# One tile of the normed rows kept in PSUM for the first mixer stage of a two-layer trunk

## The chip, the cores and the metric

The kernel runs on one core of a Trainium2 chip. The metric is the device time of one execution in microseconds (us); the median of three runs is compared. Engines are named as in the profile: PE is the matmul engine, PEld its weight load, DVE the vector engine, ACT the scalar engine, POOL GpSimd, SP the engine that only issues DMAs. A queue is written as SPq or POOLq.

## The reference, cut to what matters

The trunk has two layers over 512 positions of width 1024. Each layer sums three token mixers (A: banded attention with a learned position bias, B: a recurrent block, C: differential attention), merges them by gates, norms the result, and then runs PEER, which looks up 128 experts for each position (8 heads of 16):

```python
def peer_ffn(h, w_q, sub_keys, u, v):
    ...
    hid = jax.nn.gelu(jnp.einsum('td,thkd->thk', xb, u[experts]))
    return jnp.einsum('thk,thkd->td', g * hid, v[experts])
```

So each expert of each position costs a dot of the position's normed row `xb` with a gathered row `u` of 1024 floats, and then a weighted addition of a gathered row `v`. The scores of mixer A are

```python
    s = jnp.where(valid[None, :, None, None, :], s + bias[None, None], NEG_INF)
    p = jax.nn.softmax(s, axis=-1).astype(v.dtype)
```

## The kernel before

The sequence is cut into two halves of 256 positions, and each half runs through both layers: four phases, s = 0 to 3 (phases 0 and 1 are the halves in layer one, 2 and 3 in layer two). A half is two tiles of 128 positions, t = 0 and 1. All data are 32-bit floats.

In each phase PE, ACT and DVE go through the stages A, B, C, G (merge gates), O (output projection) and T (choice of experts). The experts' work of a phase does not end in it: part of it, gathering included, is strewn over the mixer stages of the next phase. The list `ITEMS` gives the order of all gathered rows: "P" is a pair of u and v rows, "U" and "V" single ones. `row_plan` says how many of them stand at each place of the stages. POOL runs ahead through the list and gathers each row (128 positions, 4 KB each, 512 KB in all) by an indirect DMA into a slot of a ring. In stage A the ring has 16 to 20 slots of one row. POOL waits until the slot's old row has been used.

DVE takes the rows in the same order. A "U" row is one dot, L1196, in which both inputs lie in SBUF: the gathered row and `hp[:, t, :]`, the normed rows of tile t. Stage A of phases 1 to 3 holds 76 rows: 16 ahead of its first maximum, then three behind each of the four maxima of a unit, and three behind the unit's diagonals.

Stage A has four units u of two heads. A unit has four score maps i = 2m + t (head m of the pair, tile t). PE writes a map (L629 bias, L632 scores, L635 mask), DVE takes its maximum (L1443), ACT its exponential (L953). When all four are done DVE makes the reciprocals of the sums (L1451) and four diagonal matrices (L1458), with which PE transposes and normalises the maps (L656, "weighing"); then come the outputs (L674, L676) and the q and k projection of unit u + 2 (L581 in `project_qk`). The four maps lie in four PSUM banks, 2 to 5. The V projection (L611 in `project_v`) follows the scores of unit 0. In phases 1 and 3 a map has 384 or 512 keys, in phases 0 and 2 it has 128 or 256.

The engines run their programs strictly in order:

```python
            def maxima(kind, s, u):
                ...
                for i in range(4):
                    dve.wait_ge(s_done[kind], n * 4 + i + 1)
                    v.tensor_reduce(nmax[:, u % 2, i:i + 1], sc[i][:, 0:nk(s, i % 2)], X, ALU.max, negate=True
                                    ).then_inc(smax[kind], 1)
                    rows((s, kind, u, i))
```

SP loads the weights as 512 KB panels into seven slots. Ahead of the q and k panels of unit 2 (and of unit 3) it loads a bias strip, for which it waits until all scores of unit 0 (of unit 1) are done (L498). At the end of a phase the sums of the experts' v rows lie in banks 4 to 7; DVE adds them up (L1217), and only then does PE turn the next half's rows (L593).

Of the kernel before, what the change touches and what calls it, by code (L numbers as in the profile page):

```python
# [216 lines left out]
for _n in PE_SUMS:  # L217
    GROUP_ROWS.setdefault((sum_group(_n), ITEMS[_n][4]), []).append(_n)

# [31 lines left out]
def trunk(nc, t_in, out):  # L251
    with ExitStack() as ctx:
# [113 lines left out]
        bank = [ctx.enter_context(nc.psum_tensor(f"bank{i}", [P, 512], F32)) for i in range(8)]  # L366
        sc = bank[2:6]
        tp = bank[6:8]
        pa = bank[4:8]
# [50 lines left out]
        tables = sem("tables")  # L420

# [29 lines left out]
        def nk(s, t):  # L451
            return (2 * (s % 2) + t + 1) * P
# [118 lines left out]
        def _(pe):  # L571
# [43 lines left out]
            def scores(kind, s, u):  # L615
# [7 lines left out]
                for i in range(4):  # L623
                    m, t = divmod(i, 2)
                    if u:
                        pe.wait_ge(e_done[kind], (n - 1) * 4 + i + 1)
                    k = nk(s, t)
                    if kind == "A":
                        mm(sc[i][:, 0:k], ident, strip[:, u % 2, m, STRIP - k:STRIP], start=True, stop=False)  # L629
                    rows = slice(m * HEAD_DIM, (m + 1) * HEAD_DIM)  # L630
                    for lo, hi in pairs_of(s, t):
                        mm(sc[i][:, lo:hi], qt[rows, u % 2, t * P:(t + 1) * P],  # L632
                           kt(lo // HALF, kind, u)[rows, 0:hi - lo], start=(kind == "C"),
                           stop=(kind == "C" and hi < k))
                    mm(sc[i][:, k - P:k], ident, maskblk, start=False, stop=True).then_inc(s_done[kind], 1)  # L635
# [71 lines left out]

# [174 lines left out]
        def _(act):  # L882
            fn = nc.scalar.activation
            copy = nc.scalar.copy

            def gelus(key):

                for n in rows_of(key):
                    p, kind, head, k, t = ITEMS[n]
                    c = head * TOP + k  # L890
                    if kind == "V" and n in PE_PLACE:
# [56 lines left out]
            def exps(kind, s, u, maps=range(4)):  # L948
                n = s * UNITS + u
                for i in maps:  # L950
                    k = nk(s, i % 2)
                    act.wait_ge(smax[kind], n * 4 + i + 1)
                    fn(ex[:, i * SEQ:i * SEQ + k], sc[i][:, 0:k], ACT.Exp, bias=nmax[:, u % 2, i:i + 1],  # L953
# [170 lines left out]
            for s in range(PHASES):  # L1124
                take_turned(xt, bank[0:2], x_turned, x_taken, s * 4)
# [43 lines left out]
        def _(dve):  # L1169
# [10 lines left out]
            def rows(key):  # L1180

                for n in rows_of(key):
# [12 lines left out]
                    if kind != "V":  # L1195
                        v.tensor_tensor_reduce(row, row, hp[:, t, :], 1.0, 0.0, ALU.mult, ALU.add, hid[:, t, c:c + 1]  # L1196
# [242 lines left out]
            def maxima(kind, s, u):  # L1439
                n = s * UNITS + u  # L1440
                for i in range(4):
                    dve.wait_ge(s_done[kind], n * 4 + i + 1)
                    v.tensor_reduce(nmax[:, u % 2, i:i + 1], sc[i][:, 0:nk(s, i % 2)], X, ALU.max, negate=True  # L1443
# [259 lines left out]
```

## Time and profile before

| | us |
|---|---|
| median of three runs | 3538.82 (3535.18 to 3542.63) |
| the profiled execution, its own time | 3547.76 |
| its span, first to last instruction | 3546.0 |
| busy in the span: PE, DVE, POOL, ACT | 2929.2, 2490.2, 1850.3, 832.7 |
| granted TensorE clock over the span | 0.94 of full |

Busy time alone names no bound here: the mixer stages, the choice of experts and the end have different limits, and DVE's idle time is spread over waits for DMA, PE and ACT. One has to read the stage that is changed. Stage A lies from 709 to 835 us in phase 1, from 1524 to 1645 in phase 2, from 2325 to 2450 in phase 3, and below 91 us in phase 0, where there are no rows yet.

### The profile page before, as it was taken

To read this page: it belongs to the slowest core of one execution; us is meant where nothing else is said; L and a number is where in the kernel's file an instruction comes from. 1 tells how busy PE (TensorE), PEld (TensorE's weight loads), DVE (VectorE), ACT (ScalarE), POOL (GpSimd) and SP (SyncE) were. 2 spreads that over 40 slices of the span, in tenths; PEclk is the share of its full clock that TensorE was granted. 3 is DMA by queue.
4 is the path that set the end of the run, shared out by engine and by line. 5 is a ranking of instruction groups with operands and counts; after the bars stand their busy time and mean duration, and the time that the engine had idled before them with its cause. 6 is when DMAs were issued, how large, how long until landed. Compare 5 with 4: busy or idle time off the path is not lost.

```text
span 3546.0 us, 32953 instructions
## 1 busy us (share of the span) xinstructions
PE 2929.2 (83%) x10296; PEld 1865.6 (53%) x10296; DVE 2490.2 (70%) x5295; ACT 832.7 (23%) x2384; POOL 1850.3 (52%) x1508
## 2 busy tenths in 40 slices
PE   8999788798789878886789878888789878877776
PEld 6678444266577534355477534357478434332222
DVE  1411467787887887788887877788897887754445
ACT  2310122322210123322210122322220023322222
POOL 0000044586677534588676634578677744555552
PEclk9989899999899989998889999999799989999999
DMA  4334399999899999999999999999999999999997
GB/s 162 108 95 160 105 416 420 419 367 409 325 379 409 409 412 405 421 408 408 391 395 409 408 394 407 421 371 394 373 359 409 409 417 417 415 422 421 421 421 307
DMA packets 281580, 1295.97 MB, mean 365 GB/s; under 512 B 31808, under 2 KB 32064, under 8 KB 211776
## 3 DMA queue, kind: packets, MB, share of 16 engines
q0 software_dynamic: 216576, 1073.84, 75.2%
q1 hardware_dynamic: 64256, 217.94, 16.4%
q8 instruction: 84, 1.38, 0.2%
q10 hardware_dynamic: 576, 2.10, 0.1%
q14 instruction: 88, 0.72, 0.1%
HBM read 1291.65 MB, written 2.10 MB: 365 GB/s over the span
## 4 chain that ended last, share of the span: by engine, by line
PE 44%; DMA 26%; DVE 13%; POOL 7%; issue 6%; ACT 4%; DVEq 0%; POOLq 0%; SPq 0%; ACTq 0%
PE bank L581 20%; DMA ring<-in_peer,eidx 16%; PE bank L823 11%; DMA work<-in_peer,eidx 9%; POOL ring L1163 6%; PE bank L785 4%; DVE ring L1196 3%; DVE acc L1201 3%; PE bank L656 2%; PE bank L802 2%; PE bank L632 1%; ACT dg L917 1%; DVE work L1196 1%; PE bank L611 1%; PE bank L635 1%
## 5 line engine op out<-in xcount | busy, mean ns | idle before, releaser
L1163 POOL DMA_INDIRECT ring<-in_peer,eidx x808 | 997.8, 1235 | 396.1 <-issue 219.9
L1196 DVE CUSTOM_DVE_ANT_0 ring<-ring,hp 128x1024 f32<-128x1024 f32 x816 | 984.1, 1221 | 308.7 <-DMA ring<-in_peer,eidx 308.4
L823 PE MATMUL bank<-ring,dg 128*128 128x512 f32 x1784 | 836.8, 618 | 260.7 <-ACT dg L917 228.7
L1158 POOL DMA_INDIRECT ring<-in_peer,eidx x390 | 483.5, 1240 | 934.8 <-DVE eidx L1292 437.8
L581 PE MATMUL bank<-xt,panel 128*128 128x256 f32 x4096 | 925.1, 384 | 19.7 <-ACT xt L923 5.6
L581 PEld LDWEIGHTS bank<-xt,panel 128*128 128x128 f32 x4096 | 785.2, 193 | 153.4 <-issue 30.9
L823 PEld LDWEIGHTS bank<-ring,dg 128*128 128x128 f32 x1784 | 336.4, 196 | 734.2 <-issue 694.2
L1201 DVE SCALAR_TENSOR_TENSOR acc<-ring,wgt,acc 128x1024 f32<-128x1024 f32 x326 | 415.9, 1287 | 23.0 <-DMA ring<-in_peer,eidx 21.9
L823 PE MATMUL bank<-work,dg 128*128 128x512 f32 x704 | 328.7, 611 | 110.7 <-ACT dg L917 107.6
L1196 DVE CUSTOM_DVE_ANT_0 work<-work,hp 128x1024 f32<-128x1024 f32 x208 | 252.6, 1222 | 124.3 <-DMA work<-in_peer,eidx 124.1
L1158 POOL DMA_INDIRECT work<-in_peer,eidx x154 | 187.1, 1215 | 236.9 <-PE bank L823 162.2
L823 PEld LDWEIGHTS bank<-work,dg 128*128 128x128 f32 x704 | 130.3, 193 | 295.2 <-issue 287.9
L901 ACT ACTIVATE ge<-hid 128x2 f32<-128x2 f32 x272 | 55.8, 205 | 735.5 <-DVE hid L1196 735.5
L1163 POOL DMA_INDIRECT work<-in_peer,eidx x152 | 181.7, 1195 | 85.3 <-issue 38.7
L917 ACT ACTIVATE dg<-cst,wgt 128x128 f32<-128x128 f32 x622 | 215.1, 394 | 26.5 <-PE bank L823 17.6
L656 PE MATMUL bank<-dg,ex 128*128 128x128 f32 x640 | 100.1, 322 | 100.2 <-DVE dg L1458 50.9
L785 PE MATMUL bank<-yt,panel 128*128 128x256 f32 x768 | 173.6, 379 | 0.0
L656 PEld LDWEIGHTS bank<-dg,ex 128*128 128x128 f32 x640 | 93.6, 233 | 119.9 <-issue 110.8
L785 PEld LDWEIGHTS bank<-yt,panel 128*128 128x128 f32 x768 | 145.6, 190 | 19.6
L1443 DVE TENSOR_REDUCE nmax<-bank 128x1 f32<-128x128 f32 (+3 forms) x128 | 62.4, 487 | 128.0 <-PE bank L635 128.0
L632 PE MATMUL bank<-work,qt 64*128 64x256 f32 (+1 forms) x384 | 112.4, 403 | 46.9 <-DVE work L1435 46.9
L1072 ACT ACTIVATE dg<-bank,ghalf 128x256 f32<-128x256 f32 x96 | 45.5, 474 | 392.0 <-PE bank L785 392.0
(174 smaller groups left out, 2470.0 us busy)
## 6 DMA issues: line engine op xcount, KB each, us to landing
panel<-in_panels SPq DMA_DIRECT2D x368, 512.0 KB, 6.8
ring<-in_peer,eidx POOLq DMA_INDIRECT x1198, 16.3
work<-in_rel_bias SPq DMA_DIRECT2D x16, 512.0 KB, 8.1
work<-in_peer,eidx POOLq DMA_INDIRECT x306, 21.9
gb<-in_ln_g SPq DMA_DIRECT2D x8, 512.0 KB, 8.6
gb<-in_ln_b SPq DMA_DIRECT2D x8, 512.0 KB, 10.9
panel<-in_keys SPq DMA_DIRECT2D x16, 256.0 KB, 6.2
work<-in_x SPq DMA_DIRECT2D x4, 512.0 KB, 4.6
```

Source lines behind the costliest of these rows:

```text
L581: ins = mm(dst, w[:, k * P:(k + 1) * P], rhs[:, k, :], start=(k == 0), stop=(k == n - 1))
L632: mm(sc[i][:, lo:hi], qt[rows, u % 2, t * P:(t + 1) * P], kt(lo // HALF, kind, u)[rows, 0:hi - lo], start=(kind == "C"), stop=(kind == "C" ...
L656: ins = mm(dst, ex[:, i * SEQ + j * P:i * SEQ + (j + 1) * P], dg[:, u % 2 * 4 + i, :], start=(x == maps[0]), stop=(x == maps[-1]))
L785: ins = mm(b[j][:, HALF:2 * HALF], w[:, (j * UNITS + k) * P:(j * UNITS + k + 1) * P], yt[:, c * HALF:(c + 1) * HALF], start=(k == 0), stop ...
L802: ins = mm(bank[t * 2 + n][:, :], mt[:, k, t * P:(t + 1) * P], w[:, n * 512:(n + 1) * 512], start=(k == 0), stop=(k == KC - 1))
L823: ins = mm(pa[t * 2 + half][:, :], dg[:, i % DIAGS, :], v_row[:, half * 512:(half + 1) * 512], start=(n == group[0]), stop=(n == group[-1]))
L917: fn(dg[:, i % DIAGS, :], ident, ACT.Copy, scale=wgt[:, t, c:c + 1]).then_inc(diags, 1)
L1158: pool.indirect_dma_start(slots(slot, 2), None, t_in["peer"], bass.IndirectOffsetOnAxis(ap=eidx[:, 0, t, c:c + 1], axis=0)).then_inc(row_i ...
L1163: pool.indirect_dma_start(slots(slot, 1), None, one_row, bass.IndirectOffsetOnAxis(ap=eidx[:, which, t, c:c + 1], axis=0)).then_inc(row_in ...
L1196: v.tensor_tensor_reduce(row, row, hp[:, t, :], 1.0, 0.0, ALU.mult, ALU.add, hid[:, t, c:c + 1]).then_inc(used, 1)
L1201: stt(out=acc[:, t, :], in0=row, scalar=wgt[:, t, c:c + 1], in1=acc[:, t, :], op0=ALU.mult, op1=ALU.add).then_inc(used, 1)
L1443: v.tensor_reduce(nmax[:, u % 2, i:i + 1], sc[i][:, 0:nk(s, i % 2)], X, ALU.max, negate=True).then_inc(smax[kind], 1)
```

## The change

Banks 4 and 5 hold a copy of one tile of `hp` during stage A of phases 1 to 3. ACT copies tile 0 there as soon as the sums in these banks are added up, and tile 1 when the last row of tile 0 is used. DVE reads the kept tile in place of the one in SBUF for 62 of the 64 "U" rows of heads 3 and 4 (the first two of tile 1 cover the copy and still read SBUF). For this, both heads' rows of tile 0 now come ahead of those of tile 1; they are 186 dots in three phases.

The scores of mixer A now have banks 2 and 3 alone, in all four phases. Map i may be written when map i - 2 has been read by its exponential. PE's order is changed with it: maps 0 and 1, then the V projection (unit 0) or the outputs and the next q and k projection, then maps 2 and 3. DVE's and ACT's order around the maps stays.

```diff
-    rows += u_rows(PAIR_HEADS) + u_rows(PAIR_HEADS + 1)
+    rows += [("U", head, k, t) for t in range(TILES) for head in (PAIR_HEADS, PAIR_HEADS + 1) for k in range(TOP)]
...
+def kept_tile(n):
+
+    p, kind, head, k, t = ITEMS[n]
+    if kind != "U" or KEY_OF[n][1] != "A":
+        return False
+    turn = ITEMS.index((p, "U", PAIR_HEADS + 1, TOP - 1, 0))
+    return t == 0 and n <= turn or t == 1 and n > turn + 2
...
+        hp_kept = banks[:, 4 * 512:6 * 512]
...
+        def score_bank(kind, i):
+            return bank[2 + i % 2] if kind == "A" else sc[i]
...
-                for i in range(4):
+                for i in maps:
                     m, t = divmod(i, 2)
-                    if u:
+                    if kind == "A" and (u or i >= 2):
+                        pe.wait_ge(e_done["A"], n * 4 + i - 1)
+                    elif u:
                         pe.wait_ge(e_done[kind], (n - 1) * 4 + i + 1)
...
             def stage_a(s):
                 project_qk("A", s, 0)
                 project_qk("A", s, 1)
-                scores("A", s, 0)
+                scores("A", s, 0, (0, 1))
                 project_v("A", s)
+                scores("A", s, 0, (2, 3))
                 for u in range(UNITS):
                     weigh("A", s, u)
                     if u + 1 < UNITS:
-                        scores("A", s, u + 1)
+                        scores("A", s, u + 1, (0, 1))
                     outputs("A", s, u)
                     if u + 2 < UNITS:
                         project_qk("A", s, u + 2)
+                    if u + 1 < UNITS:
+                        scores("A", s, u + 1, (2, 3))
...
+            def keep_tile(t):
+
+                for half in range(2):
+                    cols = slice(half * 512, (half + 1) * 512)
+                    ins = copy(hp_kept[:, cols], hp[:, t, cols])
+                ins.then_inc(tile_kept, 1)
...
+                    if n in TURNS:
+                        act.wait_ge(used, DVE_PLACE[n] + 1)
+                        keep_tile(1)
...
+                if s:
+                    act.wait_ge(added, 2 * s - 1)
+                    keep_tile(0)
                 take_turned(xt, bank[0:2], x_turned, x_taken, s * 4)
...
+                        normed = hp[:, t, :]
+                        if kept_tile(n):
+                            dve.wait_ge(tile_kept, 2 * p + t + 1)
+                            normed = hp_kept
```

PE's program in phase 1, unit 0, from the middle of the scores to the weighing. Before (L629, L632 and L635 write a map, 384 keys for tile 0 and 512 for tile 1; L611 is the V projection, L656 the weighing):

```order
L629 MATMUL bank<-work,cst 128x384
L632 MATMUL bank<-work,qt 128x256
L632 MATMUL bank<-work,qt 128x128
L635 MATMUL bank<-cst 128x128
L629 MATMUL bank<-work,cst 128x512
L632 MATMUL bank<-work,qt 128x256 x2
L635 MATMUL bank<-cst 128x128
L611 MATMUL bank<-panel,xt 128x512 x16
L656 MATMUL bank<-dg,ex 128x128 x14
```

The same place in the changed kernel, whose lines are numbered some 20 higher (L650, L653 and L656 a map, L630 the V projection, L677 the weighing):

```order
L630 MATMUL banks<-panel,xt 128x512 x16
L650 MATMUL banks<-work,cst 128x384
L653 MATMUL banks<-work,qt 128x256
L653 MATMUL banks<-work,qt 128x128
L656 MATMUL banks<-cst 128x128
L650 MATMUL banks<-work,cst 128x512
L653 MATMUL banks<-work,qt 128x256 x2
L656 MATMUL banks<-cst 128x128
L677 MATMUL banks<-dg,ex 128x128 x14
```

Maps 2 and 3 have moved from ahead of the V projection to behind it; nothing else stands between them and the weighing.

PE's program behind the weighing of unit 0, from map 2 of unit 1 on. Before (L674 and L676 are the outputs, L581 the projection):

```order
L629 MATMUL bank<-work,cst 128x384
L632 MATMUL bank<-work,qt 128x256
L632 MATMUL bank<-work,qt 128x128
L635 MATMUL bank<-cst 128x128
L629 MATMUL bank<-work,cst 128x512
L632 MATMUL bank<-work,qt 128x256 x2
L635 MATMUL bank<-cst 128x128
L674 MATMUL bank<-work 128x256 x3
L676 MATMUL bank<-work 128x128
L674 MATMUL bank<-work 128x256 x3
L676 MATMUL bank<-work 128x128
L581 MATMUL bank<-xt,panel 128x256 x16
```

The same stretch of the changed kernel (L695 and L697 the outputs, L600 the projection):

```order
L695 MATMUL banks<-work 128x256 x3
L697 MATMUL banks<-work 128x128
L695 MATMUL banks<-work 128x256 x3
L697 MATMUL banks<-work 128x128
L600 MATMUL banks<-xt,panel 128x256 x16
L650 MATMUL banks<-work,cst 128x384
L653 MATMUL banks<-work,qt 128x256
L653 MATMUL banks<-work,qt 128x128
L656 MATMUL banks<-cst 128x128
L650 MATMUL banks<-work,cst 128x512
L653 MATMUL banks<-work,qt 128x256 x2
L656 MATMUL banks<-cst 128x128
```

Maps 2 and 3 of unit 1 now follow the outputs and the projection of unit 2, and the weighing of unit 1 comes right behind them.

ACT's program in phase 1 of the changed kernel, where unit 1 begins (L995 takes the weighed maps of unit 0, L987 is an exponential, L914 the copy of tile 1, L1004 the outputs):

```order
L995 COPY work<-banks 128x384
L987 ACTIVATE ex,esum<-banks,nmax 128x384
L914 COPY banks<-hp 128x512 x2
L987 ACTIVATE ex,esum<-banks,nmax 128x512
L987 ACTIVATE ex,esum<-banks,nmax 128x384
L987 ACTIVATE ex,esum<-banks,nmax 128x512
L1004 COPY yt<-banks 64x256 x2
```

The copy of tile 1 stands between the exponentials of maps 0 and 1, where the activation of head 3's dots was before.

## Rows read from the trace of the kernel before

**Rows 1.** Windows over stage A and a part of stage G, phase 1; columns in the header.

```profile
core 0: us, PE busy (x) PEld busy (x) DVE busy (x) ACT busy (x) POOL busy (x), PEclk, DMA share, GB/s
709.00:835.00 126.00, 108.74 (x481) 78.78 (x482) 107.63 (x194) 34.26 (x76) 101.72 (x77) 0.95 0.98 380
...
1005.00:1100.00 95.00, 95.00 (x450) 83.84 (x449) 75.38 (x111) 12.59 (x23) 72.09 (x62) 1.00 1.03 409
```

**Rows 2.** Timeline of POOL in stage A: start, duration, instruction, idle before.

```profile
717.11 1.98 POOL L1163 DMA_INDIRECT ring<-in_peer,eidx  x1 [0.30 <-issue]
...
754.60 0.94 POOL L1163 DMA_INDIRECT ring<-in_peer,eidx  x1 [0.30 <-issue]
```

**Rows 3.** Timeline of DVE, phase 1, units 0 and 1.

```profile
738.23 0.55 DVE L1443 TENSOR_REDUCE nmax<-bank 128x1 f32<-128x384 f32 x1
...
746.16 0.15 DVE L1451 RECIPROCAL rinv<-esum 128x2 f32<-128x2 f32 x1
...
757.34 0.56 DVE L1443 TENSOR_REDUCE nmax<-bank 128x1 f32<-128x384 f32 x1 [6.43 <-PE bank L635]
...
773.22 0.16 DVE L1451 RECIPROCAL rinv<-esum 128x2 f32<-128x2 f32 x1
```

**Rows 4.** Timeline of PE, phase 1, the V projection to the third weighing.

```profile
736.67 13.90 PE L611 MATMUL bank<-panel,xt 128*128 128x512 f32 x32
751.73 3.66 PE L656 MATMUL bank<-dg,ex 128*128 128x128 f32 x28 [1.16 <-ACT work L946]
...
763.73 1.46 PE L674 MATMUL bank<-work 128*128 128x256 f32 x6
...
766.76 7.07 PE L581 MATMUL bank<-xt,panel 128*128 128x256 f32 x32
774.04 3.63 PE L656 MATMUL bank<-dg,ex 128*128 128x128 f32 x28 [0.21 <-DVE dg L1458]
...
801.19 4.83 PE L656 MATMUL bank<-dg,ex 128*128 128x128 f32 x28 [5.07 <-DVE dg L1458]
```

**Rows 5.** What PE waited for from 905 to 1005 us, stage C of phase 1.

```profile
PE bank L632 <- DVE work L1435: 15.2, 1, 15.2
```

**Rows 6.** DVE (first two) and PE, timelines of phase 2, stage A.

```profile
1556.15 0.28 DVE L1443 TENSOR_REDUCE nmax<-bank 128x1 f32<-128x128 f32 x1
...
1563.56 0.16 DVE L1451 RECIPROCAL rinv<-esum 128x2 f32<-128x2 f32 x1
...
1567.62 1.60 PE L656 MATMUL bank<-dg,ex 128*128 128x128 f32 x12 [1.16 <-ACT work L946]
...
1575.44 7.07 PE L581 MATMUL bank<-xt,panel 128*128 128x256 f32 x32
1585.95 2.90 PE L656 MATMUL bank<-dg,ex 128*128 128x128 f32 x12 [3.44 <-DVE dg L1458]
...
1615.65 2.90 PE L656 MATMUL bank<-dg,ex 128*128 128x128 f32 x12 [13.26 <-DVE dg L1458]
```

**Rows 7.** What DVE waited for from 1524 to 1645 us, stage A of phase 2.

```profile
DVE ring L1196 <- DMA ring<-in_peer,eidx: 9.3, 10, 2.3
```

**Rows 8.** Timeline of PE, phase 3, first and third weighing of stage A.

```profile
2369.50 3.66 PE L656 MATMUL bank<-dg,ex 128*128 128x128 f32 x28 [1.16 <-ACT work L946]
...
2416.26 3.63 PE L656 MATMUL bank<-dg,ex 128*128 128x128 f32 x28 [2.37 <-DVE dg L1458]
```

**Rows 9.** Timelines of phase 0: PE's V projection, DVE's last diagonals of unit 0.

```profile
34.02 13.90 PE L611 MATMUL bank<-panel,xt 128*128 128x512 f32 x32
...
35.48 0.48 DVE L1458 TENSOR_SCALAR dg<-cst,rinv 128x128 f32<-128x128 f32 x2
```

**Rows 10.** Groups by shape, 900 to 1800 us: SBUF inputs alone, and one in PSUM.

```profile
L1429 DVE TENSOR_TENSOR work<-raw,work 128x512 f32<-128x512 f32 x8 | 5.6, 697 | 0.0
...
L1431 DVE TENSOR_TENSOR work<-bank,work 128x512 f32<-128x512 f32 x8 | 5.4, 678 | 0.0
```

**Rows 11.** Time to landing of the two panels that SP issued from 1552 to 1556 us.

```profile
DMA to landing us min/median/max: 10.3/11.3/12.3
```

More of the change, by code:

```diff
@@ L218 @@
     GROUP_ROWS.setdefault((sum_group(_n), ITEMS[_n][4]), []).append(_n)
+def kept_tile(n):
[4 more added lines that the diff above has]
+    return t == 0 and n <= turn or t == 1 and n > turn + 2
+TURNS = {ITEMS.index((p, "U", PAIR_HEADS + 1, TOP - 1, 0)): p for p in range(PHASES - 1)}
 def paired(p, head):
@@ L364, in trunk @@
         iotab = sb("iotab", [P, TOP], BF16)
-        bank = [ctx.enter_context(nc.psum_tensor(f"bank{i}", [P, 512], F32)) for i in range(8)]
+        banks = ctx.enter_context(nc.psum_tensor("banks", [P, 8 * 512], F32))
+        bank = [banks[:, i * 512:(i + 1) * 512] for i in range(8)]
+        hp_kept = banks[:, 4 * 512:6 * 512]
         sc = bank[2:6]
         tp = bank[6:8]
+        def score_bank(kind, i):
+            return bank[2 + i % 2] if kind == "A" else sc[i]
         pa = bank[4:8]
@@ L420, in trunk @@
         tables = sem("tables")
+        tile_kept = sem("tile_kept")
         dve_step = sem("dve_step")
@@ L613, in project_v, with scores @@
                     ins.then_inc(panel_done, 1)
-            def scores(kind, s, u):
+            def scores(kind, s, u, maps=range(4)):
                 n = s * UNITS + u
@@ L628, in scores @@
                     if kind == "A":
-                        mm(sc[i][:, 0:k], ident, strip[:, u % 2, m, STRIP - k:STRIP], start=True, stop=False)
+                        mm(score_bank(kind, i)[:, 0:k], ident, strip[:, u % 2, m, STRIP - k:STRIP], start=True, stop=False)
                     rows = slice(m * HEAD_DIM, (m + 1) * HEAD_DIM)
                     for lo, hi in pairs_of(s, t):
-                        mm(sc[i][:, lo:hi], qt[rows, u % 2, t * P:(t + 1) * P],
+                        mm(score_bank(kind, i)[:, lo:hi], qt[rows, u % 2, t * P:(t + 1) * P],
                            kt(lo // HALF, kind, u)[rows, 0:hi - lo], start=(kind == "C"),
                            stop=(kind == "C" and hi < k))
-                    mm(sc[i][:, k - P:k], ident, maskblk, start=False, stop=True).then_inc(s_done[kind], 1)
+                    mm(score_bank(kind, i)[:, k - P:k], ident, maskblk, start=False, stop=True).then_inc(s_done[kind], 1)
             def weigh(kind, s, u):
@@ L952, in exps @@
                     act.wait_ge(smax[kind], n * 4 + i + 1)
-                    fn(ex[:, i * SEQ:i * SEQ + k], sc[i][:, 0:k], ACT.Exp, bias=nmax[:, u % 2, i:i + 1],
+                    fn(ex[:, i * SEQ:i * SEQ + k], score_bank(kind, i)[:, 0:k], ACT.Exp, bias=nmax[:, u % 2, i:i + 1],
                        accum_out=esum[:, u % 2, i:i + 1]).then_inc(e_done[kind], 1)
@@ L1195, in rows @@
                     if kind != "V":
-                        v.tensor_tensor_reduce(row, row, hp[:, t, :], 1.0, 0.0, ALU.mult, ALU.add, hid[:, t, c:c + 1]
+                        normed = hp[:, t, :]
+                        if kept_tile(n):
+                            dve.wait_ge(tile_kept, 2 * p + t + 1)
+                            normed = hp_kept
+                        v.tensor_tensor_reduce(row, row, normed, 1.0, 0.0, ALU.mult, ALU.add, hid[:, t, c:c + 1]
                                                ).then_inc(used, 1)
@@ L1442, in maxima @@
                     dve.wait_ge(s_done[kind], n * 4 + i + 1)
-                    v.tensor_reduce(nmax[:, u % 2, i:i + 1], sc[i][:, 0:nk(s, i % 2)], X, ALU.max, negate=True
+                    v.tensor_reduce(nmax[:, u % 2, i:i + 1], score_bank(kind, i)[:, 0:nk(s, i % 2)], X, ALU.max, negate=True
                                     ).then_inc(smax[kind], 1)
```

## The prediction

> **What bounds the kernel now.** I read the windows over stage A first. In phase 1 DVE is busy 108 of 126 us, PE 109, and DMA moves 380 GB/s, where a stretch of stage G that keeps it full has 409 [rows 1]. None of them is full, so the stage is a chain in which engines wait for one another. The timelines of POOL, DVE and PE show the links.
>
> POOL: a gather takes 1.98 us plus 0.30 idle while DVE runs dots back to back, and 0.94 plus 0.30 while DVE stands still [rows 2]. That is one row per two dots against one per dot. So DVE's dots hold POOL up, and in stage A this costs gathering speed.
>
> DVE and PE: in phase 1 DVE waits 6.43 us for the first map of unit 1 [rows 3], and PE later waits 5.07 us for DVE's diagonals [rows 4]. For gathered rows DVE waits little; in phase 2 it is 9.3 us in ten waits [rows 7]. In stage C PE stands 15.2 us waiting for DVE [rows 5]: DVE's program, with its rows, is what ends there. So what makes DVE stand longer in A is not absorbed in B or C, but moves everything behind it.
>
> **The change, part by part.**
>
> *The dots from PSUM, 186 of them.* No dot with a PSUM input is in the trace. The nearest rows are two elementwise operations of one shape: 697 ns with both inputs in SBUF, 678 with one in PSUM [rows 10]. From 19 ns less to 19 more for each dot is 3.5 us either way; I take 0. What does change is POOL: a gather should take 0.94 in place of 1.98 us beside such a dot. It is worth what DVE waits for rows in A, and it fills the ring earlier; beyond the ring's slots POOL must wait anyway.
>
> The Trainium skill, "SBUF — State Buffer", section "Who interferes with whom", states this: a vector instruction with two SBUF inputs contends with a GpSimd instruction that reads SBUF, one with at most one does not. The trace agrees as far as it can (1.98 against 0.94 us). The same skill speaks against the change in "VectorE: DVE Perf Modes", section on the TRN2 errata: a fixed cost of 58 cycles from SBUF and 120 from PSUM. An estimate by it is 62 cycles at 0.96 GHz, 65 ns a dot, 12 us over 186, and 3595 us for the forecast; rows 10 show no such surcharge.
>
> *The copies.* Each tile is two ACT copies of 128x512. The nearest are the two that take the V projection, for which PE waits 1.16 us [rows 4], so 1.2 us a tile. The copy of tile 0 runs while PE turns the first four blocks; ACT had no work there. DVE's first dot waits 1.2 us, but DVE stood waiting for the first map a little later in any case. The copy of tile 1 lies between two exponentials whose maxima are three dots apart (3.4 us). All of it: 0. Should ACT not be free in time, 1.2 us for each of six copies, 7 us.
>
> *Two banks, and maps 2 and 3 later.* This is the large term, since DVE takes the maxima in order with three rows behind each, and cannot pass a map that PE has not written.
>
> Pieces from phase 1. From the weighing at 751.73 to the outputs at 763.73 there are 12.0 us, 3.5 for the weighing and 8.5 for four maps, so 4.25 for two. Outputs 3.03, projection 7.07 (to the start of the next) [rows 4]. DVE reads map 0 5.6 us behind the start of the weighing [rows 3, 4], so 2.1 behind the start of that map. From the maximum of map 2 to the reciprocals are 7.9 us, and from there to the weighing 0.8 [rows 3, 4].
>
> Unit 0, phase 1: maps 0 and 1 end at 732.4. The V projection (13.9 us) comes first now, so map 2 starts at 746.3 and can be read at 748.4. DVE asks for it at 738.2: it stands 10.2 us. The weighing starts at 748.4 + 7.9 + 0.8 = 757.1, and before at 751.73: +5.4.
>
> Units 1 and 2: from weighing to weighing there are now 3.5 + 4.25 + 3.0 + 7.1 + 2.1 + 7.9 + 0.8 = 28.7 us, and PE stands idle 6.5 us before each (10.8 from the start of map 2, less 4.25 for both maps). Behind 5.07 us idle the weighing took 4.83 us, behind 0.21 it took 3.63 [rows 4], so I add 1.2: 29.9. That gives 787.0 and 816.9, where 801.19 was: **+15.7 us** in phase 1. Unit 3 has no projection ahead of its maps 2 and 3; DVE comes to map 2 later than PE writes it, so its interval stays. The waits for rows that were in these intervals are gone from this sum already: DVE stands for PE while the rows land.
>
> Phase 3 has the same shape. The first weighing moves from 2369.50 to 2374.9, the third to 2434.7 where it was at 2416.26 [rows 8]: 18.4, and 1.2 because that weighing ran at the quick 3.63: **+19.6 us**.
>
> Phase 2 has short maps. DVE asks for map 2 at 1556.15. Maps 0 and 1 end at 1550.0, the V projection at 1563.9, map 2 is readable at 1565.1: DVE stands 9 us. The reciprocals follow 7.4 later, the weighing at 1573.4 in place of 1567.62 [rows 6]. Four maps and outputs with the weighing take 7.8 (1567.62 to 1575.44); split by the matmuls that is 1.4, 5.1, 1.3. The slow weighing (2.90 against 1.60) counts again: 2.7 + 2.8 + 1.3 + 7.1 + 1.1 + 7.4 + 0.8 = 23.2 us per unit. That gives 1596.6 and 1619.8 in place of 1585.95 and 1615.65 [rows 6]: **+4.1 us**. It is small because the old interval held the 9.3 us of waits for rows [rows 7], which vanish.
>
> Phase 0 has no rows. The V projection covered the exponentials and diagonals of unit 0: the maps ended at 34.02 and the last diagonals at 35.96 [rows 9]. Now these 2 us lie bare behind map 3, in place of the 1.16 for the V copies: +1.0. In units 1 to 3 the first diagonals are ready 1.3 us behind map 3, once covered by outputs and projection: +1.3 each. **+4.9 us.**
>
> *Strips and panels.* SP waits for all maps of unit 0 before it issues the strip and then the two panels of unit 2. In phase 2 these maps now end at 1566.4, 13.9 later. The first panel lands 0.6 + 10.3 us on [rows 11], at 1577.3; PE wants it at 1580.2. Nothing to pay, with 2.9 us to spare; with the ring filling faster it may be 2 or 3 us late, twice in a phase. Phases 1 and 3 have 8 us or more.
>
> Sum: 15.7 + 19.6 + 4.1 + 4.9 = 44.3 us. On the profiled execution, 3547.8, that is 3592; it lies 9 us above the median of 3538.8, on which it gives **3583 us**, 1.25% slower.
>
> **Rivals.**
>
> (a) *POOL's freedom wins, faster.* If DMA were what ends stage A, the gathers at 0.94 us would let it run at 409 GB/s in place of 380 [rows 1]: 126 x (1 - 380/409) = 9 us in phase 1, as much in phase 3, which has the same shape, and 3539 - 18 = 3521 us. For it: rows 2. Against it: DVE must be able to go on, and the wait for map 2 is written into its program. It decides only if map 2 is written when DVE comes to it, so if DVE came 10 us later than the 738.2 of the trace. Chance 0.07. This is also what the contention rule of the skill, taken alone, promises.
>
> (b) *Part of it comes back.* While DVE stands, the ring fills, and a stretch behind that DMA ends (the choice of experts, the end of the kernel) then waits less. At most that is 16 rows of 512 KB at 409 GB/s, 1.3 us each, 20 us. Against it: stage C, where DVE's program is the bound [rows 5], fills the ring anyway. If phase 2 gives back its 4 us and phase 3 half of the 20, and the six slow weighings cost nothing (7 us), 23 us are left: 3562 us. Chance 0.13.
>
> (c) *More than the sum.* The bounds of the rows all together, 3.5 us for the dots, 7 for the copies and 6 for late panels, give 16 more: 3599 us. Chance 0.13.
>
> (d) *It does nothing,* because the new stalls hide under waits that were there (6.4 us of DVE, 5.1 of PE in phase 1). Those are in the sum already, and it would need 16 us of them. 3539 us, chance 0.03.
>
> The forecast as worked out, 3583, with 3574 to 3592 for itself, has 0.64. The range is 3562 to 3600: the lower end reaches into (b), the upper takes in (c). Within 0.2% (7 us, what a measurement of this kernel can tell from no change) counts (d) alone; faster (a); slower all others, 0.90.
>
> **What would show it.** POOL's gathers in A at about 0.94 us beside kept dots. The dots at about 1.22 us. In phase 1 DVE idle about 10 us for the third map of unit 0 and 6 to 7 us for the third map of units 1 and 2, no wait for rows. Stage A longer by some 16 and 20 us in phases 1 and 3, by 4 to 5 in 0 and 2; B, C and later as long as before. The forecast falls if the dots from PSUM differ by more than 30 ns, if A is longer but the choice of experts shorter, or if the third map is ready when DVE asks.

## The result, and the profile after

| | median of the device time, us | runs |
|---|---|---|
| before | 3540.4 (3535.2 to 3545.4) | 6 |
| changed | 3596.9 (3591.5 to 3607.5) | 6 |

The ratio is 1.0159, with a 95% interval of 1.0145 to 1.0174: the change costs 1.6%, some 56 us. The forecast was 3583, with a range to 3600. The profiled execution of the changed kernel took 3599.8 us, with a span of 3598.0; before it was 3547.8 and 3546.0, so the two traces differ by 52.0 us. In the text TensorE is PE, VectorE DVE, ScalarE ACT, GpSimd POOL and SyncE SP.

VectorE in phase 1 of the changed kernel (timeline; the maxima of unit 0's second and third map, of unit 1's first and third):

```profile
735.02 0.69 DVE L1484 TENSOR_REDUCE nmax<-banks 128x1 f32<-128x512 f32 x1
749.11 0.56 DVE L1484 TENSOR_REDUCE nmax<-banks 128x1 f32<-128x384 f32 x1 [9.98 <-PE banks L656]
...
764.54 0.56 DVE L1484 TENSOR_REDUCE nmax<-banks 128x1 f32<-128x384 f32 x1 [2.82 <-PE banks L656]
...
778.73 0.56 DVE L1484 TENSOR_REDUCE nmax<-banks 128x1 f32<-128x384 f32 x1 [6.19 <-PE banks L656]
```

The third map of unit 0 makes VectorE stand 9.98 us (749.11), that of unit 1 6.19 us (778.73). The same view shows 6.19 again for unit 2. Over the stage, by the view of waits from 709 to 853 us:

```profile
DVE nmax L1484 <- PE banks L656: 33.8, 7, 10.0
DVE ring L1237 <- ACT banks L914: 1.3, 1, 1.3
```

33.8 us in seven waits for maps, none for gathered rows. The wait of 1.3 us is the first kept dot's, for the copy. The first three of the four weighings on TensorE:

```profile
757.85 4.74 PE L677 MATMUL banks<-dg,ex 128*128 128x128 f32 x28 [6.44 <-DVE dg L1499]
787.47 5.26 PE L677 MATMUL banks<-dg,ex 128*128 128x128 f32 x28 [6.44 <-DVE dg L1499]
817.62 5.54 PE L677 MATMUL banks<-dg,ex 128*128 128x128 f32 x28 [6.44 <-DVE dg L1499]
```

TensorE stands 6.44 us before each of them, and each takes 4.7 to 5.5 us where it took 3.63 behind a short wait [rows 4]. The windows over stage A of phases 1, 2 and 3:

```profile
core 0: us, PE busy (x) PEld busy (x) DVE busy (x) ACT busy (x) POOL busy (x), PEclk, DMA share, GB/s
710.00:852.00 142.00, 112.40 (x480) 83.26 (x480) 106.75 (x194) 36.12 (x80) 77.48 (x79) 0.89 0.92 352
1546.00:1664.00 118.00, 86.45 (x344) 64.13 (x344) 95.56 (x185) 26.98 (x69) 72.92 (x75) 0.80 1.03 407
2356.00:2494.00 138.00, 108.79 (x450) 79.73 (x451) 100.24 (x187) 33.98 (x75) 72.86 (x75) 0.88 0.91 351
```

VectorE's busy time in phase 1 is what it was (106.75 us, before 107.63 [rows 1]), in a stage 16 us longer. GpSimd's fell from 101.72 to 77.48 us. The granted clock fell from 0.95 to 0.89, and the DMA engines moved less a second, 352 GB/s for 380: nothing in this stage is nearer to being full. Phase 2 is another case: there the DMA engines are as full as before, 1.03 of their time at 407 GB/s in both kernels (before: 1524 to 1645 us); yet VectorE no longer waits for a row in it. GpSimd beside sixteen kept dots (groups, 711 to 729 us), and the kept dots themselves (the page's costliest groups):

```profile
L1200 POOL DMA_INDIRECT ring<-in_peer,eidx x13 | 12.2, 939 | 6.7 <-DVE hid L1237 4.3 <-issue 2.4
```

```profile
L1237 DVE CUSTOM_DVE_ANT_0 ring<-ring,hp 128x1024 f32<-128x1024 f32 x642 | 779.4, 1221 | 290.0 <-DMA ring<-in_peer,eidx 290.0
...
L1237 DVE CUSTOM_DVE_ANT_0 ring<-ring,banks 128x1024 f32<-128x1024 f32 x174 | 202.1, 1215 | 3.9 <-ACT banks L914 3.9
```

A gather takes 0.94 us where it took 1.98 [rows 2], and a dot with an operand in PSUM 1215 ns where one from SBUF takes 1221.

Where the 52 us arose, from the timelines: stage A, from the start of TensorE's first transpose to the start of the last of its four weighings, in every profile of this study. "Late" marks traces in which some result of TensorE was taken 7 us or more after its last matmul by engines that were idle; that comes below.

| profile | chip | A, phase 0 | phase 1 | phase 2 | phase 3 | span |
|---|---|---|---|---|---|---|
| before | first | 79.7 | 116.1 | 110.1 | 112.4 | 3546.0 |
| changed | first | 88.4 | 132.4 | 115.4 | 134.7 | 3598.0 |
| banks_only | second | 86.8 | 132.6 | 119.7 | 135.3 | 3607.7 |
| scores_before_proj (late) | second | 82.7 | 138.4 | 132.9 | 138.2 | 3627.7 |
| scores_in_a_row (late) | second | 81.3 | 141.4 | 133.2 | 148.0 | 3638.3 |
| rows_before_map3 (late) | second | 88.8 | 138.1 | 134.9 | 137.9 | 3630.2 |
| before_again | third | 80.5 | 111.3 | 110.3 | 110.3 | 3540.5 |
| after_again (late) | third | 87.9 | 142.5 | 130.3 | 138.4 | 3631.2 |
| phase0_old (late) | third | 79.5 | 142.3 | 131.5 | 145.2 | 3634.4 |
| maps_first_sbuf | third | 82.7 | 119.4 | 108.5 | 119.2 | 3569.9 |
| after_third | fourth | 88.3 | 132.3 | 117.0 | 136.7 | 3594.1 |
| banks_only_again | fourth | 90.9 | 131.9 | 114.0 | 134.6 | 3585.2 |
| copies_only | fourth | 87.6 | 133.0 | 117.2 | 136.8 | 3590.9 |
| kept_paced | fourth | 88.3 | 132.6 | 117.4 | 134.9 | 3598.9 |

In the first pair the four stages A are longer by 8.7, 16.3, 5.3 and 22.3 us, 52.6 in all. Outside them 7.7 us came back in the rest of phase 0, and 2.4 and 4.7 were lost between the stages A of phases 1, 2 and 3. (One of the three later chips may be the first again; a ratio compares runs on one chip.)

### The profile page after: what moved, and what is told of

Read it like the earlier page. It is cut to its first block, busy times and chain, and to the rows that moved or that the text cites. A ratio compares the mean times of both kernels' runs of the same rounds, so it can differ in the third digit from the quotient of the medians.

```text
span 3598.0 us, 33164 instructions
## 1 busy us (share of the span) xinstructions
PE 2941.5 (82%) x10296; PEld 1880.5 (52%) x10296; DVE 2486.9 (69%) x5295; ACT 838.4 (23%) x2396; POOL 1770.0 (49%) x1508
## 3 DMA queue, kind: packets, MB, share of 16 engines
q1 hardware_dynamic: 64256, 217.94, 16.3%
## 4 chain that ended last, share of the span: by engine, by line
PE 50%; DMA 25%; DVE 14%; issue 6%; ACT 4%; POOL 1%; DVEq 0%; POOLq 0%; SPq 0%; ACTq 0%
PE banks L600 22%; DMA ring<-in_peer,eidx 19%; PE banks L847 11%; DMA work<-in_peer,eidx 6%; DVE ring L1237 5%; PE banks L809 4%; PE banks L677 3%; DVE acc L1242 2%; PE banks L630 2%; PE banks L653 2%; PE banks L826 2%; PE banks L656 1%; ACT dg L951 1%; POOL ring L1195 1%; PE banks L695 1%
## 5 line engine op out<-in xcount | busy, mean ns | idle before, releaser
L847 PE MATMUL banks<-ring,dg 128*128 128x512 f32 x1784 | 837.6, 618 | 260.3 <-ACT dg L951 233.7
L1237 DVE CUSTOM_DVE_ANT_0 ring<-ring,hp 128x1024 f32<-128x1024 f32 x642 | 779.4, 1221 | 290.0 <-DMA ring<-in_peer,eidx 290.0
L600 PE MATMUL banks<-xt,panel 128*128 128x256 f32 x4096 | 921.3, 383 | 19.7 <-ACT xt L957 5.6
L600 PEld LDWEIGHTS banks<-xt,panel 128*128 128x128 f32 x4096 | 782.6, 192 | 152.1 <-issue 30.8
L847 PEld LDWEIGHTS banks<-ring,dg 128*128 128x128 f32 x1784 | 336.5, 196 | 734.7 <-issue 698.9
L847 PE MATMUL banks<-work,dg 128*128 128x512 f32 x704 | 329.0, 611 | 116.6 <-ACT dg L951 104.2
L847 PEld LDWEIGHTS banks<-work,dg 128*128 128x128 f32 x704 | 131.0, 194 | 300.6 <-issue 284.7
L951 ACT ACTIVATE dg<-cst,wgt 128x128 f32<-128x128 f32 x622 | 215.0, 394 | 26.5 <-PE banks L847 17.6
L677 PE MATMUL banks<-dg,ex 128*128 128x128 f32 x640 | 112.7, 352 | 132.3 <-DVE dg L1499 85.6
L1237 DVE CUSTOM_DVE_ANT_0 ring<-ring,banks 128x1024 f32<-128x1024 f32 x174 | 202.1, 1215 | 3.9 <-ACT banks L914 3.9
L677 PEld LDWEIGHTS banks<-dg,ex 128*128 128x128 f32 x640 | 106.5, 262 | 147.5 <-issue 145.2
L809 PE MATMUL banks<-yt,panel 128*128 128x256 f32 x768 | 173.6, 379 | 0.0
L809 PEld LDWEIGHTS banks<-yt,panel 128*128 128x128 f32 x768 | 145.6, 190 | 19.6
L653 PE MATMUL banks<-work,qt 64*128 64x256 f32 (+1 forms) x384 | 115.4, 412 | 47.0 <-DVE work L1476 47.0
```

The costliest lines, as they stand in the source:

```text
L600: ins = mm(dst, w[:, k * P:(k + 1) * P], rhs[:, k, :], start=(k == 0), stop=(k == n - 1))
L653: mm(score_bank(kind, i)[:, lo:hi], qt[rows, u % 2, t * P:(t + 1) * P], kt(lo // HALF, kind, u)[rows, 0:hi - lo], start=(kind == "C"), sto ...
L677: ins = mm(dst, ex[:, i * SEQ + j * P:i * SEQ + (j + 1) * P], dg[:, u % 2 * 4 + i, :], start=(x == maps[0]), stop=(x == maps[-1]))
L809: ins = mm(b[j][:, HALF:2 * HALF], w[:, (j * UNITS + k) * P:(j * UNITS + k + 1) * P], yt[:, c * HALF:(c + 1) * HALF], start=(k == 0), stop ...
L847: ins = mm(pa[t * 2 + half][:, :], dg[:, i % DIAGS, :], v_row[:, half * 512:(half + 1) * 512], start=(n == group[0]), stop=(n == group[-1]))
L951: fn(dg[:, i % DIAGS, :], ident, ACT.Copy, scale=wgt[:, t, c:c + 1]).then_inc(diags, 1)
```

## The experiments

Four kernels on the second chip, where before ran in 3558.8 us. They take the change apart and move the late third map.

**banks_only.** No kept tile, no copies, the rows in their old order; TensorE's new order and two banks stay.

```
-    rows += [("U", head, k, t) for t in range(TILES) for head in (PAIR_HEADS, PAIR_HEADS + 1) for k in range(TOP)]
+    rows += u_rows(PAIR_HEADS) + u_rows(PAIR_HEADS + 1)
...
-                    if n in TURNS:
-                        act.wait_ge(used, DVE_PLACE[n] + 1)
-                        keep_tile(1)
...
-                if s:
-                    act.wait_ge(added, 2 * s - 1)
-                    keep_tile(0)
...
-                        if kept_tile(n):
-                            dve.wait_ge(tile_kept, 2 * p + t + 1)
-                            normed = hp_kept
```

> This kernel has the two score banks and TensorE's new order, but no kept tile: the dots read the normed rows in SBUF, ScalarE makes no copies, and the rows have the order of before. Theory: the whole loss is the third and fourth score maps that TensorE issues behind V's projection, the outputs and the next projection, while VectorE takes its rows in an unchanged order. Then this kernel is as slow as the changed one, 3590 to 3602 us, with VectorE idle about 10 us ahead of the third map of unit 0 and 6 us ahead of that of units 1 and 2 in phases 1 and 3. Rival 1, the kept dots or ScalarE's twelve copies cost something (7 us at most by the copies' own time): 3585 to 3590. Rival 2, the kept dots give time back (gathers at 0.94 in place of 1.98 us in stage A): 3605 or more.

Measured: 3606.0 us, ratio 1.0137 (1.0117 to 1.0158). VectorE's waits for maps in stage A of phase 1 come to 34.8 us (24.9 put down to TensorE, and one of 9.9 for which the view names no releaser), and in the repeat further down to 33.7 in seven, where the changed kernel has 33.8. So the loss is there without the kept tile.

**scores_before_proj.** The third and fourth map ahead of the projections.

```
-                scores("A", s, 0, (0, 1))
+                scores("A", s, 0)
                 project_v("A", s)
-                scores("A", s, 0, (2, 3))
...
                     outputs("A", s, u)
+                    if u + 1 < UNITS:
+                        scores("A", s, u + 1, (2, 3))
                     if u + 2 < UNITS:
                         project_qk("A", s, u + 2)
-                    if u + 1 < UNITS:
-                        scores("A", s, u + 1, (2, 3))
```

> The whole change, kept tile and two banks, but TensorE issues the third and fourth map ahead of the next unit's projection (behind the outputs), and for unit 0 ahead of V's projection. Theory: VectorE then finds the third map ready when it comes to it, since the 7 us of projection (14 us of V) no longer lie before it; TensorE waits instead for the exp of the maps before, one to three us a unit, part of which lies under time that it had idle anyway. The time goes back to 3540 to 3556 us. Rival: what costs is having two banks at all, TensorE's waits for the exps, in whatever order: 3570 to 3600 us.

Measured: 3628.4 us, ratio 1.0186 (1.0165 to 1.0207), worse than either expectation. Its timeline shows VectorE's part as I expected and something else besides:

```profile
783.00 0.55 DVE L1483 TENSOR_REDUCE nmax<-banks 128x1 f32<-128x384 f32 x1
...
784.49 7.07 PE L600 MATMUL banks<-xt,panel 128*128 128x256 f32 x32
...
799.00 0.38 ACT L966 ACTIVATE qt<-banks 128x256 f32<-128x256 f32 x1 [9.98 <-remote]
...
800.19 3.35 PE L677 MATMUL banks<-dg,ex 128*128 128x128 f32 x14 [4.60 <-ACT work L994]
```

The third map (783.00) is ready when VectorE asks. But TensorE's projection ends at 791.56, and ScalarE, idle, takes it at 799.00, 7.4 us late; "remote" says that the trace shows no releaser. In the next unit the projection ends at 822.06, and ScalarE takes it at 829.25. SyncE, which waits for the same count before it issues a panel, issues one at 829.24: so it isn't ScalarE that was slow, what both wait for came late, although the trace has TensorE at the weighing from 822.22 us on. TensorE's later weighings wait behind it.

**scores_in_a_row.** All four maps in a row, as before the change, with two banks.

```
-                scores("A", s, 0, (0, 1))
+                scores("A", s, 0)
                 project_v("A", s)
-                scores("A", s, 0, (2, 3))
...
                     if u + 1 < UNITS:
-                        scores("A", s, u + 1, (0, 1))
+                        scores("A", s, u + 1)
...
-                    if u + 1 < UNITS:
-                        scores("A", s, u + 1, (2, 3))
```

> The whole change, but TensorE issues the four maps in a row as before the change, ahead of the outputs (and of V's projection for unit 0), with two banks: so it stands still until the exp of map 1, behind three rows on VectorE, has left its bank. Theory: TensorE's stop is some 5 us a unit (three rows of 1.2 us, two maxima and an exp), its work some 19 us a unit; the sum of about 24 is VectorE's own cycle, so the time is 3542 to 3565 us, at most a few us above the kernel with the maps behind the outputs. Rival, TensorE's stop adds to its path in full (5 us in four units of two phases): 3575 to 3600 us.

Measured: 3636.4 us, 1.0211 (1.0179 to 1.0243). Late again, by 8.9 us at the first projection of phase 1 and 11.7 in phase 3.

**rows_before_map3.** TensorE's order as changed; VectorE's rows moved.

```
-                    plan += [((s, stage, u, i), k) for i, k in enumerate(spread(n, 5))]
+                    parts = [3, 9, 1, 1, 1] if stage == "A" else spread(n, 5)
+                    plan += [((s, stage, u, i), k) for i, k in enumerate(parts)]
```

> The whole change with TensorE's new order kept; what is moved are VectorE's rows of stage A: 3, 9, 1, 1, 1 behind the four maxima and the diagonals of a unit, where they were 3, 3, 3, 3, 3. Theory: TensorE's late third map costs only because VectorE has nothing but its maximum to take next; with six more rows (7 us) ahead of it VectorE's idle time there falls from 6.2 to about 0 in units 1 and 2 and from 10 to 3 in unit 0, and the exps of maps 2 and 3 follow without rows between them, so that the weighing starts earlier by as much. The time is 3535 to 3560 us. Rival: the third map's lateness is on TensorE's own path (weighing, outputs, projection, third map, exp, diagonal, weighing), with no slack for VectorE's order to use: 3575 to 3597 us.

Measured: 3636.7 us, 1.0225 (1.0205 to 1.0245). VectorE waits 3.13 us for the third map of unit 0, as expected, but 4.73 and 2.41 in units 1 and 2. In unit 1 it read the map 26.5 us behind the start of the weighing before it, in the changed kernel 20.9; 3.1 us of this passed after the map's last matmul. What the move is worth stays open.

All three had the kept tile and many late takings. banks_only, without the tile, had one: in phase 2 its transposes end at 1554.44 us and the last copy starts at 1558.55, 4.1 us late. So the next four, on a third chip, began with controls.

**before_again**, the kernel before.

> The kernel before, unchanged, for its profile on the chip that the next three share. In the three kernels with an earlier third map or moved rows, ScalarE took a projection 4 to 9 us after TensorE's last matmul of it by the records, at 730 us and again in units 2 and 3 of phase 1; the kernel before was 18 us slower on that chip than on its first. Theory 1, such late takings come with the chip: they then stand in this profile too if its span is again near 3565. Theory 2, they come with what those kernels change: none stands here, and the takings in phase 1 follow within 0.2 us as in the first profile.

One run, 3542.3 us; before ran in 3547.9 us on this chip. The projections of phase 1 are taken at once. Only at the start of stage A in phase 2 are copies late (transposes that end at 1519.70, their copies at 1521.65 and 1523.10, so 1.9 and 3.4 us).

**after_again**, the changed kernel.

> The changed kernel, unchanged, on the same chip as the others of this call: a ratio of 1.014 to 1.018 again to before. If it is 1.020 or more on this chip, the kernels with an earlier third map were no slower than it; if 1.016, they lost 0.3 to 0.6% against it although TensorE no longer makes VectorE wait. The projections of phase 1 are taken within 0.2 us if late takings don't come with the chip.

Measured: 3637.7 us, ratio **1.0258** (1.022 to 1.0295), for 1.0159 in the result. Here it has the late takings too. Phase 2, timeline of ScalarE and TensorE where stage A begins:

```profile
1560.38 1.06 PE L612 MATMUL banks<-cst,work 128*128 128x128 f32 x8 [2.68 <-issue]
1561.36 1.07 ACT L957 COPY xt<-banks 128x512 f32<-128x512 f32 x2
1562.08 1.94 PE L612 MATMUL banks<-cst,work 128*128 128x128 f32 x8 [0.64 <-ACT xt L957]
...
1566.20 0.58 ACT L957 COPY xt<-banks 128x512 f32<-128x512 f32 x1 [3.78 <-remote]
...
1577.38 0.58 ACT L957 COPY xt<-banks 128x512 f32<-128x512 f32 x1 [10.60 <-remote]
1578.02 9.36 PE L600 MATMUL banks<-xt,panel 128*128 128x256 f32 x32 [14.01 <-issue]
```

The transposes end at 1564.02; their last copy starts at 1577.38, and the first projection waits for it. In the changed kernel's first profile the four copies follow within 3.5 us:

```profile
1547.07 0.59 ACT L957 COPY xt<-banks 128x512 f32<-128x512 f32 x1
1547.92 0.59 ACT L957 COPY xt<-banks 128x512 f32<-128x512 f32 x1 [0.27 <-PE banks L612]
1548.92 1.25 ACT L957 COPY xt<-banks 128x512 f32<-128x512 f32 x2 [0.41 <-PE banks L612]
1557.43 0.38 ACT L967 ACTIVATE qt<-banks 128x256 f32<-128x256 f32 x1 [7.26 <-PE banks L600]
```

**maps_first_sbuf.** The order of scores_before_proj, dots from SBUF, rows as before the change: what is left of the change is that there are two banks.

> Two banks; the third and fourth map ahead of the projection (of V's for unit 0); no kept tile and no copies: dots read SBUF, rows in the old order. Theory: the kept dots free GpSimd's gathers (0.94 us each), which fill the DMA engines (1.02 to 1.05 of their time at 700 to 740 and 814 to 832 us in the kernel with the kept tile and the same order), and something in that makes the late takings; with dots from SBUF the gathers are slower, the late takings are gone, and the time is within 0.4% of before, 1.000 to 1.004. Rival: the order alone makes them: 1.015 to 1.020 as with the kept tile.

Measured: 3562.7 us, ratio **1.0041** (1.0021 to 1.0061). Timelines of VectorE and TensorE, phase 1:

```profile
740.53 0.69 DVE L1474 TENSOR_REDUCE nmax<-banks 128x1 f32<-128x512 f32 x1
744.57 0.55 DVE L1474 TENSOR_REDUCE nmax<-banks 128x1 f32<-128x384 f32 x1
...
772.82 0.56 DVE L1474 TENSOR_REDUCE nmax<-banks 128x1 f32<-128x384 f32 x1 [15.56 <-PE banks L656]
...
780.76 0.55 DVE L1474 TENSOR_REDUCE nmax<-banks 128x1 f32<-128x384 f32 x1
```

```profile
742.09 1.70 PE L650 MATMUL banks<-work,cst 128*128 128x512 f32 x2 [1.25 <-ACT ex L983]
746.31 15.40 PE L630 MATMUL banks<-panel,xt 128*128 128x512 f32 x32
...
789.53 3.63 PE L677 MATMUL banks<-dg,ex 128*128 128x128 f32 x28 [0.17 <-DVE dg L1489]
...
811.82 3.63 PE L677 MATMUL banks<-dg,ex 128*128 128x128 f32 x28 [0.21 <-DVE dg L1489]
```

No third map is waited for (744.57, 780.76). The price of two banks in phases 1 and 3 is TensorE's 1.25 us for an exponential, once in each; in phase 2 it waits four times for one, 9.5 us in all. The second and third weighing follow their diagonals within 0.2 us and take 3.63 us again. Unit 1's first map is late instead (15.56 us): the V projection took 15.40 us, and the map's last matmul ended at 768.99, while VectorE, idle, read it at 772.82. So a map taken 3.8 us late is here too, without a kept tile. The four stages A are 17.4 us longer than those of before_again on the same chip (11.5 against before's first profile), where the changed kernel's were 52.6 us longer; this profiled execution was 9 us over its kernel's median.

**phase0_old.** The whole change, but phase 0 with four banks and the old order.

```
-    return bank[2 + i % 2] if kind == "A" else sc[i]
+    return bank[2 + i % 2] if kind == "A" and s else sc[i]
...
-                scores("A", s, 0, (0, 1))
+                scores("A", s, 0, (0, 1) if s else range(4))
```

> The whole change, but phase 0, which has no rows, keeps four banks and the old order. Theory: phase 0's loss of 8.6 us in stage A came back by the end of the phase, since TensorE ran at a higher granted clock afterwards, and only 0.9 us reached phase 1. The time is that of the changed kernel, less 0 to 1.5 us (ratio lower by 0.0003). Rival, the loss was repaid by chance of clock: 4 to 9 us less (ratio lower by 0.001 to 0.0025).

Measured: 3631.3 us, 1.0219 (1.0182 to 1.0256), 6.4 us under after_again by the medians, the intervals overlapping. Stage A of phase 0 has its 79.5 us again, and phase 1 begins at 708.7 us in place of 715.7. That is the rival's case, but it isn't settled: before_again has the same phase 0 on the same chip and began phase 1 at 700.6 us, 8.1 earlier, so what follows stage A in phase 0 varies by as much as the loss.

The last four, on a fourth chip (before 3542.0 us), were to split the kept tile's cost.

**after_third**, the changed kernel.

> The changed kernel, unchanged, for its time and profile on the chip of the next three. Its ratio was 1.016 on one chip and 1.026 on another; it is either of the two, or between. Where it is over 1.020, ScalarE takes the first projections of stage A in phases 1 to 3 late by 1.7 to 7.4 us against TensorE's last matmul of them, as on the second chip; where 1.016, not.

Measured: 3597.6 us, 1.0171 (1.0137 to 1.0205), no late takings in this kernel nor in the three that follow.

**banks_only_again.**

> Two banks and the new order of TensorE; no kept tile, no copies, rows in the old order. 1.012 to 1.016 whatever the chip, if the kept tile alone makes the difference between chips; the same ratio as the changed kernel's, within 0.002, if it is something else that comes with the chip.

Measured: 3589.7 us, 1.0142 (1.0112 to 1.0173).

**copies_only.** One line less: `normed = hp_kept`.

> The changed kernel with its copies, its order of rows and its waits, but the dots read the normed rows in SBUF: the two PSUM banks are filled and nothing reads them. If the copies and the order of rows are free, as I predicted, this is the kernel without a kept tile: 1.012 to 1.016. If what costs on the second chip is the dots' operand in PSUM or the gathers that it frees, the changed kernel is above this by 0.010 and this one is at 1.014. Rival, the copies or the order of rows cost: this one is at the changed kernel's ratio.

Measured: 3599.3 us, 1.0167 (1.0138 to 1.0196). Beside its first dots GpSimd is slow again (groups, 711 to 729 us):

```profile
L1200 POOL DMA_INDIRECT ring<-in_peer,eidx x11 | 17.2, 1562 | 3.4 <-issue 3.0 <-DVE hid L1236 0.3
```

Yet its time is the changed kernel's. Reading the tile from PSUM, with all that it gives GpSimd (1562 to 939 ns a gather), is worth nothing that can be measured.

**kept_paced.** Half as many gathers beside the first sixteen kept dots.

```
                     else:
+                        first, last = RANGE[KEY_OF[old]]
+                        if kept_tile(old) and KEY_OF[old][2] == -1:
+                            old = min(2 * old - first, last - 1)
                         pool.wait_ge(used, DVE_PLACE[old] + 1)
```

> The changed kernel, but of the gathers that reuse the slots of the first sixteen kept rows of stage A, each waits for twice as many dots, so that eight are issued beside the sixteen dots and eight after them, about as with dots from SBUF (1.98 us each), in place of sixteen. If the rush of gathers at the start of stage A makes the late takings (DMA engines at 1.02 to 1.03 of their time from 700 to 740 us), they are gone and the ratio is within 0.003 of the copies-only kernel, 1.012 to 1.018. If the operand in PSUM makes them, the ratio is the changed kernel's on this chip.

Measured: 3597.8 us, 1.0155 (1.0122 to 1.0187). On a chip without late takings it can't tell what makes them. It does show again that the early gathers bring nothing: with 8 of them in place of 13 from 711 to 729 us the time is the same.

## Why the prediction held, point by point

The mechanism held, and the ratio that it gave (1.25%) was short of the 1.6% measured. That the time lies in the range is in part luck of the chip: on the third one the same kernel is 2.6% slower than before, on the second its relatives with the kept tile 1.9 to 2.3%, and the range ended at 1.7%. The prediction had no term for the late takings that go with these.

**What bounds the kernel.** A chain of engines that wait for one another, as read from the windows. In stage A of phases 1 and 3 of the changed kernel every engine and the DMA engines are less full, and it is longer.

**The dots, 0 us.** Right: 1215 for 1221 ns. The Trainium skill ("VectorE: DVE Perf Modes", on the TRN2 errata) has a fixed cost of 120 cycles from PSUM against 58 from SBUF, which I estimated at 12 us; this difference isn't seen in this instruction. The measurement decides.

**The gathers, 0.94 us.** Right (939 ns), as the contention rule of the Trainium skill has it ("SBUF — State Buffer", "Who interferes with whom"). Their worth was to be what VectorE waits for rows in A; it is shown by copies_only: none that can be measured.

**The copies, 0 us.** Not shown either way. The three kernels with copies and the new order of rows took 3597.6, 3599.3 and 3597.8 us, the one without 3589.7; the intervals overlap. Its stages A of phases 1 to 3 are 4.4 to 6.5 us shorter, about my upper bound (7 us), so some us may belong here. But ScalarE not being free in time isn't seen for tile 1: with the copy of tile 1 between them the exponentials of maps 0 and 1 start 4.03 us apart (765.13 and 769.16 in the changed kernel), without it 4.04 (763.07 and 767.11 in banks_only_again). Behind the copy of tile 0 the first projection starts 4.1 to 4.3 us after the first transpose (after_third, phases 1 to 3), without it 3.2 to 3.7 in banks_only_again, but 4.0 to 4.3 in the kernel before. Of the difference 3 us lie between the first two weighings of phase 2, 25.9 us in after_third and 23.0 in banks_only_again, where TensorE's maps took 0.79 us each for 0.48; in banks_only on the second chip this interval was 24.2.

**Maps 2 and 3, phases 1 and 3.** This carries the forecast, and each step is in the rows: VectorE idle 9.98 and 6.19 us (forecast 10.2, then 6 to 7), TensorE idle 6.44 before each weighing (6.5), 29.6 and 30.2 us between weighings (29.9), and in phase 1 +16.3 us (15.7). Phase 3 was +22.3 for 19.6: 2.0 us of the rest came ahead of the first weighing, where its first projection took 9.49 us for 7.17 before, and 0.7 behind the third, which took 5.55 us where I had counted 4.83. That the order in which TensorE issues these maps is the cause is shown by maps_first_sbuf, which differs from banks_only in this order alone: 1.0041 in place of 1.0137 and 1.0142. The three ratios come from three chips; that of maps_first_sbuf comes from one with late takings, so it isn't flattered by them. So of the loss some 1.0% is the order, 0.4% what is left with two banks in the better order, and up to 0.3%, not surely above nothing, the copies and rows.

**Phase 2, +4.1 us.** +5.3; close, but in part by luck. VectorE stood 8.80 us for the third map (forecast 9), and its waits for rows are gone, as I said. The first weighing came 3.8 us later in the stage and not 5.8, and the two intervals behind it took 26.1 and 23.5 us for 23.2 each.

**Phase 0, +4.9 us.** Under-sized: +8.7. The bare times are there: TensorE waits 2.08 us before the first weighing for 1.16 before (my 2 us less 1.16 is 0.8, not the 1.0 that I wrote; it is 0.9), and 1.20 us before the other three. But TensorE then ran at a lower granted clock, 0.95 where it had 1.00 from 28 to 91 us. In the first pair 7.7 us of it were gone by phase 1; in phase0_old against after_again they were not. Two profiles of the kernel before begin phase 1 at 709.1 and 700.6 us, so one pair can't settle 8 us there.

**B, C and the rest "as long as before".** Nearly. In stage C of phase 2 some 4.2 us came on top, from its first map to its last weighing: the maps of its second unit took 0.79 and 1.22 us for 0.49 and 0.70, with a granted clock of 0.73 from 1740 to 1822 us, where before had 0.77 in the same part of the stage (1715 to 1792). I had no term for that.

**The strips and panels, 0 us.** Nothing contradicts it: TensorE waits for no panel in either trace.

**Rivals.** (a) fell: the gathers are fast, and useless. (b) fell: from stage A of phase 1 on, nothing was given back. (c) was nearer to the truth than I made it, 3596.9 for its 3599, but by other items: not the dots and panels, but phases 0 and 3, stage C, and perhaps the copies. The sum was 12 us short, inside the range; 8 of them show in the pair of traces, the rest is that before's profiled execution lay 7 us over its median and the changed kernel's 3. (d) fell.

## What to carry to other kernels

When a buffer is halved, what costs need not be the buffer: see which consumer takes the second half in order, and what the producer issues ahead of it. Here 14 us of projection ahead of the third map cost a stall in the consumer, a stall back in the producer, and a slower clock on top. Freeing an engine (GpSimd: 24 us less busy in one stage) helps nothing if no wait in the program ends on it. And before a small gain is believed, the pair should run on more than one chip.

## What the runs showed that was not expected

On two of the four chips TensorE's results are taken late: every engine that waits for them stands idle after TensorE's last matmul of them by the trace, while VectorE's dots and GpSimd's gathers go on. With dots from SBUF this is up to 3.4 us, at one place, in the kernel before, 4.1 us once in banks_only, and 3.8 in maps_first_sbuf, where ScalarE takes a weighed map 5.6 us late beside it. With the kept tile it is up to 14 us, at the start of stage A and behind projections, and on the third chip the changed kernel is 2.6% slower than before in place of 1.6%. On the other two chips no kernel shows it, kept tile or not.

So the chip, or what came with it, has a part in it, and the kernels with the kept tile fare worse. Whether by their reads of PSUM, by the gathers that these free, by the copies or by the order of rows was not told apart, since copies_only and the paced kernel ran where there was nothing to remove. Full DMA engines alone don't make it: from 700 to 740 us they are at 1.02 of their time in after_again and in the changed kernel's first profile alike. Nor is it settled that only the signals are late. The profile models the ends of matmuls, and in after_again two matmuls of one map (L650) start at 2408.61 and 2410.04 us, with 2.42 and 0.41 us idle before them for which the trace names no releaser, so TensorE itself may have been held up. The late takings also hid, in the first four experiments, what the order was worth.
